# A two-layer RWKV / diff-attention / expert network on one core: the first expert tile among the projections, every eighth row added on GpSimd, and new orders in recurrence and attention

## The reference, cut to what matters

```
g     = sigmoid(gd) @ g_up                         # layer 0, rwkv7_mix
out_a = (((o - mean) * rsqrt(var + eps)) * ln_w + ln_b + bonus) * g

h  = rms(x) * (1 + scale) + shift                  # after x = x + gate * (y @ w_out)
q  = (h @ w_q).reshape(p, 8, 2, 128)               # 8 heads
s  = einsum('phmd,mnd->phmn', q, sub_keys)         # two times 128 scores
sv, si = top_k(s, 16)                              # then top 16 of the 16 x 16 sums
g  = softmax(best)
act = gelu(einsum('phkd,pd->phk', u_tab[eidx], h)) # 16 rows of u a head and token
out = einsum('phk,phkd->pd', g * act, v_tab[eidx]) # and 16 rows of v
```

## Time and profile before

| | us |
|---|---|
| median of 3 runs | 3152.46 (3149.62 to 3152.9) |
| the profiled execution, its own time | 3153.75 |
| its span in the profile | 3151.9 |
| PE busy in the span | 2648.8 (84%) |
| DVE busy | 2096.0 (66%) |
| POOL busy | 1079.8 (34%) |
| ACT busy | 683.9 (22%) |
| TensorE's mean granted clock | 0.966 |
| bytes moved by DMA | 926.98 MB, 294 GB/s in the mean |

### The profile page before, as it was taken

How to read it: one execution, slowest core, us unless ns; L and a number is a source line. 1 busy time by engine, 2 the same in 40 slices (tenths; PEclk the granted TensorE clock), 3 DMA queues, 4 the chain that set the end, 5 groups by cost and what they waited for, 6 DMA issues and landing times. The chain is left out here.

```text
span 3151.9 us, 31365 instructions
## 1 busy us (share of the span) xinstructions
PE 2648.8 (84%) x9264; PEld 1315.9 (42%) x9264; DVE 2096.0 (66%) x4860; ACT 683.9 (22%) x1707; POOL 1079.8 (34%) x927
## 2 busy tenths in 40 slices
PE   6996999997899998777777777777977788877776
PEld 2442888884444443222222222223444344432222
DVE  2335333435567777888888888886575677778886
ACT  2134333331122211111111111111024222111111
POOL 0002323222144444444444444441000334444443
PEclk9998999998999999999999999999998899999999
DMA  5233000005499999999999999997422699999997
GB/s 191 80 143 141 1 1 1 1 1 229 174 395 405 400 400 400 420 421 420 417 420 421 421 415 419 420 420 303 175 69 102 280 420 420 420 413 419 420 420 323
DMA packets 137150, 926.98 MB, mean 294 GB/s; under 512 B 16960, under 2 KB 17984, under 8 KB 31576
## 3 DMA queue, kind: packets, MB, share of 16 engines
q0 software_dynamic: 113664, 822.20, 63.6%
q1 hardware_dynamic: 23392, 103.57, 8.8%
HBM read 924.59 MB, written 1.11 MB: 294 GB/s over the span
## 5 line engine op out<-in xcount | busy, mean ns | idle before, releaser
L1545 PE MATMUL psum<-ring,diag 128*128 128x512 f32 x3072 | 1488.9, 619 | 357.7 <-DVE diag L1665 356.6
L1423 POOL DMA_INDIRECT ring<-in_uv,experts x768 | 915.6, 1192 | 1274.8 <-PE psum L1545 1033.2
L1719 DVE CUSTOM_DVE_ANT_0 ring<-ring,hcur 128x1024 f32<-128x1024 f32 x768 | 941.3, 1226 | 307.5 <-DMA ring<-in_uv,experts 279.9
L1545 PEld LDWEIGHTS psum<-ring,diag 128*128 128x128 f32 x3072 | 554.7, 193 | 1204.2 <-DVE diag L1665 735.2
L1453 ACT ACTIVATE gel<-dots 128x1 f32<-128x1 f32 x768 | 148.8, 201 | 1421.4 <-DVE dots L1719 1419.8
L1665 DVE TENSOR_SCALAR diag<-ident,gel,wcur 128x128 f32<-128x128 f32 x768 | 257.6, 345 | 19.1 <-ACT gel L1453 19.1
L1135 DVE COPY_PREDICATED T<-level,psum 128x512 f32<-128x512 uint32 x80 | 58.6, 733 | 173.9 <-PE psum L900 173.9
L418 PE MATMUL psum<-zT,win_ring 128*128 128x512 f32 x368 | 162.1, 601 | 5.2 <-PEq L90 5.2
L1785 PE MATMUL psum<-wqkv_ring,zT 128*128 128x512 f32 x320 | 139.3, 598 | 2.9 <-PEq L90 2.9
L1524 PE MATMUL psum<-yT,w_q 128*128 128x512 f32 (+1 forms) x256 | 121.3, 576 | 2.5 <-issue 2.5
L418 PEld LDWEIGHTS psum<-zT,win_ring 128*128 128x128 f32 x368 | 70.5, 193 | 91.8 <-issue 91.8
(11 more groups left out here) (390 smaller groups left out, 2667.2 us busy)
## 6 DMA issues: line engine op xcount, KB each, us to landing
wmod<-in_w_mod SPq DMA_DIRECT2D x32, 1024.0 KB, 7.6
w_q<-in_w_q SPq DMA_DIRECT2D x36, 512.0 KB, 8.0
wmod<-in_w_mod POOLq DMA_DIRECT2D x16, 1024.0 KB, 5.5
ring<-in_uv,experts POOLq DMA_INDIRECT x768, 10.8
wqkv_ring<-in_w_qkv SPq DMA_DIRECT2D x6, 2048.0 KB, 9.9
win_ring<-in_w_in SPq DMA_DIRECT2D x23, 512.0 KB, 3.6
w_all<-in_w_o SPq DMA_DIRECT2D x8, 512.0 KB, 7.2
scores<-in_w_out SPq DMA_DIRECT2D x6, 512.0 KB, 5.6
```

The lines of the kernel that those rows point to most:

```text
L1423: nc.gpsimd.indirect_dma_start(ring[:, s % RING], None, uv, bass.IndirectOffsetOnAxis(ap=experts[:, n, j:j + 1], axis=0)).then_inc(row_in[ ...
L1545: m = nc.tensor.matmul(ps[:, c], diag[:, j % DIAGS], ring[:, j % RING, D + 512 * c:D + 512 * c + 512], start=(first and j == 0), stop=(las ...
L1719: nc.vector.tensor_tensor_reduce(u, u, hcur[:], 1.0, 0.0, ALU.mult, ALU.add, dots[:, j:j + 1]).then_inc(dot_done, 1)
```

## The change

In `out_and_experts` (both layers, unless NT is named):

- TensorE projects tile 0 and the first half of tile 1, transposes tile 0, and makes query, scores of head 0, query, scores of head 1, before it finishes tile 1's projection. Tiles 2 and 3 are projected later, the last behind row 3 of unit 0.
- VectorE routes head 0 before `out(1)` and `norm(1)`. `out` and `norm` of tiles 2 and 3 stand inside unit 0, at rows 6 and 8. ACT's `root` and `turned` follow.
- Unit 0's queries for head 2 stand at rows 6 to 13, and no more at 0 to 12.
- For layer 0's first tile (`POOLED`, NT = 4) the rows j = 7 and 15 of each unit get no diag and no matmul. POOL multiplies the row in the ring by gelu times weight and adds it to `pooled` in SBUF, ahead of the gather that reuses the slot; `mm_done` and `diag_done` are raised by two with the row before. VectorE adds `pooled` to the tile's sum at its end.

In `rglru` TensorE takes each modulation chunk one unit sooner and reduces it two chunks late; ACT copies it before the roots; VectorE adds the rows later. In `rwkv_finish` ACT takes the square, the gate is made transposed, and bias and gate are applied in one VectorE operation on the transposed data; `ln_b` is loaded as a column of 128 by 4 (`shift`). In `attention` VectorE takes `maxima(u + 2)` before `copy_out(u - 1)`.

```diff
 # out_and_experts, gpsimd
+                def accumulate(n, j):
+                    pool.wait_ge(gelu_done, n * TOPK + j + 1)
+                    pstep(nc.gpsimd.tensor_tensor(pw[:], gel[:, j:j + 1], weights[:, n, j:j + 1], ALU.mult))
+                    v = ring[:, j % RING, D:]
+                    pstep(nc.gpsimd.tensor_scalar(v, v, pw[:], None, ALU.mult))
+                    last = nc.gpsimd.tensor_tensor(pooled[:], pooled[:], v, ALU.add)
+                    pstep(last)
...
+                        if RING <= s < HEADS * TOPK + RING and POOLED(j):
+                            accumulate((s - RING) // TOPK, (s - RING) % TOPK)
                         if s >= RING:
                             pool.wait_ge(mm_done, DIAGS + s - RING + 1)
 # scalar, ahead of the units
-                for i in range(2, NT):
-                    turned(i - 1)
-                    root(i)
-                turned(NT - 1)
+                root(1)
                 act.wait_ge(max_done, 1)
                 nc.scalar.activation(ex[:], best[:], ACT.Exp, bias=nmax[:], accum_out=total[:]).then_inc(exp_done, 1)
+                turned(1)
+                for j in range(TOPK):
+                    if NT > 2 and j == FIRST_QUERY:      # 6
+                        root(2)
+                    if j == EXP_AT:                      # 8
+                        if NT > 2:
+                            turned(2)
+                            root(3)
+                            turned(3)
...
 # tensor
                 project(0)
-                project(1)
+                project(1, 0, KD // 2)
                 turn(0)
...
+                project(1, KD // 2, KD)
+                if NT > 2:
+                    project(2)
+                turn(1)
+                for j in range(TOPK):
+                    if NT > 2 and j == 4:
+                        project(3)
+                        turn(2)
+                    if NT > 2 and j == FIRST_QUERY:
+                        turn(3)
+                    if j == FIRST_QUERY:
+                        pe.wait_ge(ev_done, 2 * NT)
+                    m, ks = FIRST_PART(j)
+                    if ks:
+                        query(AHEAD, m, 0, *ks)
...
+                    if POOLED(j):
+                        continue
+                    pe.wait_ge(diag_done, j + 1)
 # vector
                     for j in range(TOPK):
+                        if NT > 2 and isinstance(n, int) and n == 0 and j in (FIRST_QUERY, EXP_AT):
+                            out(2 if j == FIRST_QUERY else 3)
+                            norm(2 if j == FIRST_QUERY else 3)
 # add(0)
+                            dve.wait_ge(pooled_done, 1)
+                            tstep(tt(sums[:], sums[:], pooled[:], ALU.add))
 # rglru, tensor
-                    if n >= 1:
-                        add_groups(n - 1)
+                    if n >= 2:
+                        add_groups(n - 2)
...
-                    if u >= 2:
-                        mod_groups(u - 2)
+                    if u >= 1:
+                        mod_groups(u - 1)
 # rglru, scalar
+                    if u >= 1:
+                        copy_part(u - 1)
                     if u in ROOTS_AT:
...
-                    if u >= 2:
-                        copy_part(u - 2)
 # rglru, vector
                 for u in range(5, 8):
                     scan(u)
-                    mod_row(u)
+                    mod_row(u - 1)
+                mod_row(7)
 # rwkv_finish, scalar and vector
+                nc.scalar.activation(sq[:], O[:], ACT.Square).then_inc(sq_done, 1)
+                for c in range(4):
+                    act.wait_ge(g_mm, c + 1)
+                    nc.scalar.activation(gT[:, c], ps[:, c], ACT.Copy).then_inc(gt_done, 1)
...
-                step(tt(O[:], O[:], row(2), ALU.add))
...
+                    nc.vector.scalar_tensor_tensor(yT[:, c], ps[:, 4 + c], shift[:, c:c + 1], gT[:, c],
+                                                   ALU.add, ALU.mult).then_inc(ev_done, 1)
 # rwkv_finish, sync
+                sp.dma_start(shift[:], a["rows"][0, 4].rearrange("(c p) -> p c", p=P), allow_slow_non_contiguous=True).then_inc(shift_in, 16)
 # attention, vector
-                    if u >= 1:
-                        copy_out(u - 1)
                     if u + 2 < NU:
                         maxima(u + 2)
+                    if u >= 1:
+                        copy_out(u - 1)
```

More of the change, by code:

```diff
@@ L1287, in _ @@
                 pe.wait_ge(c_in, 32)
-                for t in range(TILES):
-                    nc.tensor.matmul(ps[:, t], sg[:, t * P:(t + 1) * P], g_up[:], start=True, stop=True).then_inc(g_mm, 1)
+                for c in range(4):
+                    nc.tensor.matmul(ps[:, c], g_up[:, c * P:(c + 1) * P], sg[:], start=True, stop=True).then_inc(g_mm, 1)
                 pe.wait_ge(scol_ready, 1)
@@ L1545, in unit, with project @@
                             m = nc.tensor.matmul(ps[:, c], diag[:, j % DIAGS], ring[:, j % RING, D + 512 * c:D + 512 * c + 512],
-                                                 start=(first and j == 0), stop=(last and j == TOPK - 1), skip_group_check=True)
-                        m.then_inc(mm_done, 1)
-                def project(i):
+                                                 start=(first and j == 0), stop=(last and j + take == TOPK), skip_group_check=True)
+                        m.then_inc(mm_done, take)
+                def project(i, k0=0, k1=KD):
                     if i >= 2:
                         pe.wait_ge(ps_read, 2 * (i - 1))
-                    for k in range(KD):
+                    for k in range(k0, k1):
                         pe.wait_ge(w_in[k], 16)
@@ L1587, in _ @@
                     i.then_inc(q_mm, 2)
-                pe.wait_ge(k_in, 16)
-                for head in range(AHEAD):
+                    if head == 0:
+                        pe.wait_ge(k_in, 16)
                     pe.wait_ge(q_done, 2 * head + 2)
@@ L1703, in _ @@
                     route_part(first, 0, part)
-                for i in range(2, NT):
-                    out(i)
-                    norm(i)
+                out(1)
+                norm(1)
                 route_part(first, 0, 9)
```

128 lines of the change are left out of this document (78 added, 50 removed).

## The result

The changed kernel takes 3162.4 us (median of 7 runs, 3158.2 to 3166.5), the kernel before 3152.5 beside it; the ratio is 1.0027, interval 1.0018 to 1.0037. It is 9.9 us slower where I had forecast 27 less. The profiled execution took 3164.05, span 3162.2.

A forecast was written before the change was run, and what follows sets the result against it. DMA was taken to set most expert units, TensorE those of layer 0's first tile. Terms -8 - 1 - 5.5 - 1.6 - 7.3 - 4.3 = -27.7 gave 3126.0, less 1.3, say 3125 us; range 3107 to 3146.

The forecast's parts named there:

- (d): Layer 0's first tile, the seven units after unit 0: 306.6 us against 308.2 before, -1.6.
- my chain: GpSimd's queue in layer 0's first tile: pooled row and the gathers behind it, 21.9 us per eight rows, 43.8 a unit.
- my bounds of the unit: Length of a pooled unit in layer 0's first tile: 42.5 us (-10.7 in all) to 47.7 us (+25.7).
- 45 to 48: Case of pooled units between 45 and 48 us, kernel at 3134 to 3150 us; chance 0.08.
- third rival: Layer 0's pooled tile: GpSimd's queue bounds it all, `tensor_scalar` at twice 2.9 us, units 49.8, +42, kernel 3167; chance 0.07.
- first rival: Layer 0's pooled tile: GpSimd's part is hidden, DMA sets units at 42.5 us, 9.1 less, kernel 3116; chance 0.21.
- (a): Recurrence (`rglru`): TensorE's wait for ACT's copy goes, the load of `wmod` is late next; -8 us, bounds 0 and -12.
- (c): Start of layer 0's experts: first gather 9.3 us earlier, query weights late, unit 0 done 5.5 us earlier; bounds -9 and 0.
- (b): `rwkv_finish`: VectorE's shorter list leaves GpSimd freer, the small load delays it; -1 us, bounds -3 and +2.
- (e): Attention: maxima ahead cover VectorE's 0.72 us wait, 13 units x 0.56 = -7.3 us, bounds -10 and -2.
- (f): Layer 1's experts: first gather 9.3 us earlier, 5 us given back to loads beside it; -4.3 us, bounds -9 and 0.
- second rival: Recurrence and attention reorders pay little, scans and the round over TensorE being the chain; kernel 3139 us; chance 0.14.

The follow-up runs named there:

- a_queue9: Changed kernel with GpSimd's two wide operations per pooled row replaced by nine of one element, pooled rows left out of the sum; 3143.9 us, ratio 0.9965.
- np_port: Changed kernel with no row pooled, GpSimd doing a 256-element `tensor_scalar` on its own data behind each gather in layer 0's first tile; 3153.4 us.
- best1: Changed kernel with the recurrence's `mod_row` ahead of the next unit's gate products and layer 0's experts as before the change; 3129.7 us, ratio 0.9923.
- a_rec_fix: Changed kernel with one recurrence line moved: VectorE's `mod_row(u - 4)` ahead of the next unit's gate products; 3146.5 us, ratio 0.9978.
- a_mid: Changed kernel with the two pooled rows of a unit at j = 3 and 11 in place of 7 and 15; 3170.9 us, ratio 1.0057.
- a_queue_only: Changed kernel with GpSimd's two wide operations per pooled row replaced by 20 of one element, pooled rows left out of the sum; 3254.6 us, ratio 1.0321.
- a_half: Changed kernel with one row of 16 pooled, the last of each unit (j = 15), not two; 3165.1 us, ratio 1.0035.

## Why the prediction was wrong

(d), the seven units, is the largest miss: -1.6 forecast, +16.3 measured. I had two paths, GpSimd's queue (43.8) and VectorE's (42.7 to 44.8), and took the unit as the longer of them. What failed is the step that built both with VectorE's and TensorE's work as it was before: in the queue's chain dots at 1.3, diags at 0.35 and a product at 1.7 us. Measured, the sharing costs 2.2 to 2.6 us a unit on top of the queue's hold (a_queue9), and np_port shows it from the other side, +1.9. I had put it at nothing there beyond GpSimd's own waits. The product was mis-sized as well: I had let TensorE lose 3.4 us a unit at a clock of 1.00, and its busy time fell by 1.7, since with its new waits the clock fell to 0.50 for some 34 us. My 7.5 us for the pooled row was too much, not too little: the hold is 6.6 in the mean.

That both of my paths gave 43.8, and that a_queue9 took 43.8, is chance. With a_queue9's hold of 6.0 in place of 7.5 my chain gives 20.4 us per eight rows, 40.8 a unit, and the measured one is 3 us longer; what sets it is open. VectorE's path was wrong in the other direction: I let GpSimd's work block it for 8.5 to 10.6 us a unit, and it was busy only 3.5 longer (36.0 against 32.6). It waited 51.0 / 6 = 8.5 us, so its own path is 37.9 and not 42.7 to 44.8. The average unit of 46.4 lay within my bounds of the unit, but I gave 45 to 48 a chance of 0.08. The third rival had the sign, but its mechanism is not shown: the `tensor_scalar` took 2.8 to 3.9, not 5.8. Against it I had said that a scalar costs less than a tensor; the earlier trace rows had it the other way (1500 against 1278 ns), and so did the pooled row (2.84 against 2.35). A slip besides: 5 x 44.62 + 42.35 + 42.96 is 308.4, not 308.2.

The first rival fell with it, and so did the Trainium skill's rule behind it (GPSIMD Engine Reference, section 4.1 Engine selection, one-input operations "roughly line-rate"): the `tensor_scalar` over 1024 elements took 2.84 us at its shortest, nearly twice the 1.50 over 512 of the earlier trace rows, and not the 1.1 estimated by that rule. The trace does not agree.

(a), the recurrence: -8 forecast, +6.1 measured. The step "so that wait goes" held, "what is late next is the load of `wmod`" did not (its waits were 0.17 and 1.26 us): late next was VectorE's `mod_row(u - 4)`. I had looked at whom the moved sum waits for on ACT, not at its second wait, for the row that frees its PSUM bank. That row stood behind `gated(u + 1)`, thus behind gates issued just before the wait, and the gates of the unit after stood behind the wait: a full round over three engines per unit. With that one line moved, the stage is 6.7 (best1) to 9.6 us (a_rec_fix) shorter than before, about the -8 forecast. That size is in part luck: seven steps of 5 us from 222 end at 257, not at the 250 of my sum. In a_rec_fix the seven steps, from 218.79 to 246.85, took 4.0 each, so two errors cancelled.

(c), the head of layer 0: -5.5 forecast, -0.5 measured to gather 22. The first query matmul came at 870.36, which in the old kernel's time is 863.7, forecast 863; the first gather 8.0 us earlier, forecast 9.3. The end of the sum failed in two places. The first four records of the query took 3.75 us, four later ones 1.88, because the granted clock was 0.50 there (870.36 to 874.20), as it was before (847.16 to 850.90); I had all 32 at the full clock. And I had read the gain at the end of unit 0 on TensorE (897.5 before, now 902.0, which is 895.3 in the old kernel's time, so -2.2). Gather 22 shows less, because it waits for row 14, which is now the unit's last product. With no row pooled the head is 2.4 us longer than before: what gain I had came from two rows fewer for TensorE in that unit, not from the order. Then +4.4 us from gather 134 on, where I had "costs nothing; if not, 6": the pooled row at the tile's end and the addition of `pooled` do cost, and without pooling +0.4 is left; the two were not taken apart.

(b) -1.3 for -1; with the same code this stage took 35.8 to 37.7 us in the runs (before 38.9), and none of them takes its parts one by one. (e) -10.6 for -7.3: the mechanism held, a unit takes 2.98 us (forecast 3.05), but the gain comes in all 16 units, not in 13: 16 x 0.63 = 10.1. Changed kernel, VectorE, one unit after the other:

```profile
2386.55 0.34 DVE L2106 SCALAR_TENSOR_TENSOR o<-psum,inv,sub_g 128x128 f32<-128x128 f32 x1
2388.20 1.22 DVE L2101 TENSOR_REDUCE nmax<-psum 128x2 f32<-128x1024 f32 x1
...
2389.53 0.34 DVE L2106 SCALAR_TENSOR_TENSOR o<-psum,inv,sub_g 128x128 f32<-128x128 f32 x1
```

(f) -5.9 for -4.3: the first gather comes 42.2 us behind the stage's start, before 51.2, so 9.0 earlier (forecast 9.3), and 3 of them are given back, not 5. The second rival, that the reorders pay little, was right for the recurrence and wrong for attention. `rwkv_scan`'s +1.8 was in no term; over the runs it lies between 433.6 and 436.5 with one code, so it is spread.

## What to carry to other kernels

When a wait is moved, list all semaphores of the waiting instruction and look where each releaser stands in its engine's order relative to the work queued behind the wait. Work given to a second engine that delays the first is not hidden by the idle time of either: count the delay into every chain in which an operation of the first stands, and ask which of its operations fall beside the new work. Taking work from TensorE buys less than its length if it then waits and its clock falls: here 1.7 of 3.4 us a unit. An earlier start of loads was worth nothing in a stretch that TensorE nearly fills, and some 6 us in layer 1, where the gathers themselves are the limit. Redo a sum that agrees with a measurement: here two 43.8 agreed by chance.

## What the runs showed of the hardware

GpSimd's wide operations and VectorE's delay each other. In np_port VectorE's dots took 1264 ns instead of 1224, and GpSimd's operation on 256 elements 1129 ns on average and 0.94 us at the shortest. In the changed kernel a dot beside a 2.35 us `tensor_tensor` took 3.13, and the pooled `tensor_scalar` 2.84 to 3.9. Not all of VectorE's operations suffer: `hot` (two tensors, 512 elements) went from 692 to 2732 ns in a_mid, while the operation just ahead of it (`hot<-hl,iota`, 512 elements), beside the same pooled row, took 678 against 684.

A chain of operations on one element on GpSimd takes 0.51 to 0.53 us for each on average, in a row of 9 or 20 (508 ns in a_queue9, 534 in a_queue_only); the shortest was 0.28.

TensorE's granted clock fell from 1.00 to 0.50 (1.2 GHz) with a wait of 3.82 us in the changed kernel (up to 998.86) and with one of 3.08 us in a_half (up to 1000.06), in stretches in which TensorE was otherwise busy. It did not with each such wait: with the same 3.08 us, up to 1047.44 in a_half, it stayed at 1.00.
